# Neighbourhood attention: project queries and keys of both head pairs first, then run one pipeline of attention steps

## What is computed

```python
def na_project(p, qk_gain):
    q = rms_norm(p[0].reshape(B, T, NA_HEADS, HEAD_DIM), qk_gain[0])
    k = rms_norm(p[1].reshape(B, T, NA_HEADS, HEAD_DIM), qk_gain[1])
    v = p[2].reshape(B, T, NA_HEADS, HEAD_DIM)
...
    # for each grid row: queries against a window of 8 x 16 grid keys and all context keys
    s_loc = jnp.einsum('bchd,brcjhd->bhcrj', q_r, k_w).astype(jnp.float32) * NA_SCALE + bias
    s_ctx = jnp.einsum('bchd,bkhd->bhck', q_r, k_ctx).astype(jnp.float32) * NA_SCALE
    p = jax.nn.softmax(jnp.concatenate([s_loc, s_ctx], -1), axis=-1)
    out = p_loc @ v_w + p_ctx @ v_ctx
```

## Time and profile before

| | |
|---|---|
| Median of 3 runs | 2172.21 us (2169.93 to 2174.93) |
| The profiled execution | 2174.71 us, of which the span of the trace is 2172.9 |
| TensorE (PE) busy | 2046.5 us, 94% |
| Weight loads (PEld) | 1689.9 us, 78% |
| VectorE (DVE) busy | 1139.5 us, 52% |
| ScalarE (ACT) busy | 757.2 us, 35% |
| GpSimd (POOL) busy | 645.1 us, 30% |
| Layer 0, neighbourhood attention with its queries and keys | about 60 to 178 us of the span |
| Layer 1, the same | about 1290 to 1389 us |

### The profile page before, as it was taken

One profiled execution on the slowest core, in us unless ns is written; L12 is line 12 of the kernel. 1 busy time (PEld: TensorE's weight loads), 2 busy tenths in 40 slices (PEclk: granted clock), 3 DMA queues, 4 the chain that ended last, 5 costly groups with the idle time before them and its releaser, 6 DMA issues.

```text
span 2172.9 us, 29749 instructions
## 1 busy us (share of the span) xinstructions
PE 2046.5 (94%) x11694; PEld 1689.9 (78%) x11694; DVE 1139.5 (52%) x1975; ACT 757.2 (35%) x1209; POOL 645.1 (30%) x820
## 2 busy tenths in 40 slices
PE   7889999999989999999999998889989989999999
PEld 5777888766668888888888877688866667888887
DVE  5455433578866666277537564654368864212111
ACT  4443232546653211111111244433366643222222
POOL 1111221210002433343333431122220014555555
PEclk8999999999999999999999999997999999999999
DMA  7302431100002333233223210111110002333323
GB/s 295 114 20 72 154 97 40 48 30 10 10 11 68 112 121 100 75 129 133 88 97 117 97 59 30 32 49 40 49 49 10 10 21 78 97 97 97 99 95 107
DMA packets 76528, 166.24 MB, mean 77 GB/s; under 512 B 5224, under 2 KB 46824, under 8 KB 75376
## 3 DMA queue, kind: packets, MB, share of 16 engines
q1 hardware_dynamic: 75728, 163.18, 22.5%
q10 hardware_dynamic: 672, 1.25, 0.2%
HBM read 162.31 MB, written 2.10 MB: 76 GB/s over the span
## 4 chain that ended last, share of the span: by engine, by line
PE 81%; DVE 7%; ACT 4%; issue 4%; DMA 1%; PEld 1%; POOL 1%; SPq 0%; PEldq 0%; DVEq 0%; ACTq 0%; POOLq 0%
PE psum L1156 23%; PE psum L1157 22%; PE psum L1158 22%; PE psum L1415 1%; DMA wm<-w_mod 1%; PE psum L1769 1%; PE psum L1207 1%; ACT nap L771 1%; PE psum L1799 1%; PE psum L1406 1%; POOL wlo L584 1%; PE psum L1538 1%; PE psum L1475 1%; PE psum L1524 1%; PE psum L1476 1%
## 5 line engine op out<-in xcount | busy, mean ns | idle before, releaser
L584 POOL TENSOR_TENSOR wlo<-raw,whi 128x256 fp32r<-128x256 f32 x816 | 644.9, 822 | 1519.8 <-ACT whi L609 1519.8
L1156 PE MATMUL psum<-hhi,whi 128*128 128x512 f32 (+1 forms) x1704 | 611.5, 359 | 15.5 <-DVEq L1970 8.3
L1157 PE MATMUL psum<-hlo,whi 128*128 128x512 f32 (+1 forms) x1704 | 601.3, 353 | 0.0
L1158 PE MATMUL psum<-hhi,wlo 128*128 128x512 f32 (+1 forms) x1704 | 600.7, 353 | 0.0
L609 ACT ACTIVATE whi<-raw 128x1024 fp32r<-128x1024 f32 x204 | 215.6, 1058 | 870.9 <-PE psum L1158 864.2
L1156 PEld LDWEIGHTS psum<-hhi,whi 128*128 128x128 f32 x1704 | 325.5, 191 | 69.9 <-issue 13.5
L1158 PEld LDWEIGHTS psum<-hhi,wlo 128*128 128x128 f32 x1704 | 324.7, 191 | 44.5
L1157 PEld LDWEIGHTS psum<-hlo,whi 128*128 128x128 f32 x1704 | 325.5, 191 | 42.0 <-issue 0.5
L2621 DVE TENSOR_TENSOR ffuf<-ffsa,psum 128x768 f32<-128x768 f32 (+1 forms) x44 | 36.1, 821 | 312.7 <-ACT ffsa L1106 306.0
L2606 DVE SCALAR_TENSOR_TENSOR ffmacc<-wm,csil,ffmacc 128x256 f32<-128x256 f32 x336 | 188.6, 602 | 10.0 <-DVE ffmacc L2606 4.9
L1156 PE MATMUL psum<-uhi,whi 128*128 128x512 f32 (+1 forms) x528 | 188.4, 357 | 3.7 <-DVE ulo L2625 2.1
(11 more groups left out here) (323 smaller groups left out, 3064.5 us busy)
## 6 DMA issues: line engine op xcount, KB each, us to landing
raw<-w_stream SPq DMA_DIRECT2D x204, 512.0 KB, 3.5
wm<-w_mod SPq DMA_DIRECT2D x80, 512.0 KB, 4.0
wm<-w_mod SPq DMA_DIRECT2D x8, 1024.0 KB, 13.1
xres<-x_t SPq DMA_DIRECT2D x8, 384.0 KB, 7.2
out<-xres SPq DMA_DIRECT2D x8, 256.0 KB, 2.7
namask<-c_f ACTq DMA_DIRECT2D x2, 384.0 KB, 3.7
consts<-c_f SPq DMA_DIRECT2D x1, 254.0 KB, 2.8
narpb<-rpb ACTq DMA_DIRECT2D x2, 120.0 KB
```

Source lines behind the costliest of these rows:

```text
L584: nc.gpsimd.tensor_tensor(wlo[:, q % 2, c:c + UW // 4], raw[:, q % RAW, c:c + UW // 4], whi[:, q % 2, c:c + UW // 4], ALU.subtract).then_i ...
L1156: mm(dst, ah, bh, start=first, stop=False)
L1157: mm(dst, ah, bl, start=False, stop=False)
L1158: return mm(dst, al, bh, start=False, stop=last)
```

## The change

Queries and keys of pair 1 are projected right behind those of pair 0, and both barriers between the pairs go. Then a single pipeline runs over the steps of both pairs: 24 in layer 0 and 16 in layer 1.

- `qhi`, `qlo`, `khi` and `klo` hold both pairs (`[P, 2, TOK]`), and steps carry their pair `pr`. To make room the tiles of the stage are laid out anew: `sq`, `t` and `vt` share the place of the outputs' neighbours, and `r`, `mask` and `ks` share another; two unused gaps shrink or move.
- `na_second` replaces `na_pair`. TensorE multiplies the grid part of unit 4, then the sums of pair 0's key squares, then the context part of unit 4 (layer 0), the grid part of unit 5, the sums of pair 1's query squares, the context part of unit 5, the sums of pair 1's key squares, and then the 40 filler matmuls, now into bank 5. Pair 1's keys go to PSUM pair 0 and its query sums to PSUM pair 3.
- A new semaphore `na_scaled` is counted up by VectorE when a query or key has been scaled out of PSUM. TensorE waits for it before unit 4 (pair 0's queries), before pair 1's query sums (pair 0's keys) and before the filler (pair 1's queries). ScalarE waits for it before the roots of pair 1.
- ScalarE rounds unit 5 before the roots of pair 0's keys instead of behind them, and squares pair 1's queries before it rounds unit 6.
- SyncE's two waits for a phase count become 2 and 4, since two barriers of a layer are gone.

```diff
@@ -307,7 +305,7 @@
                     steps = []
                     for kind, t in att_blocks(l):
                         for a in range(2):
-                            steps.append((s, b, kind, t, a))
+                            steps.append((s, b, kind, t, a, pr))
                             s += 1
                         b += 1
                     plan[l, pr] = steps
...
@@ -345,6 +343,10 @@
         def NAQK(l, pr, part):
 
             return 3 * (2 * l + pr) + ("q", "kx", "kc").index(part) + 1
+
+        def SCALED(l, pr, part):
+
+            return 4 * l + 2 * pr + ("q", "k").index(part) + 1
 
         NAK_PARTS = (("kx", slice(CTX_LEN, TOK)), ("kc", slice(0, CTX_LEN)))
 
...
@@ -548,14 +550,14 @@
             for h in range(2 * MOD_HEAD, 2 * MOD_GATE):
                 load_mod(0, h)
             loads(RAW, ML_G + RAW)
-            sp.wait_ge(pe_phase, 4)
+            sp.wait_ge(pe_phase, 2)
             for n in range(MOD_GATE, MODC):
                 for h in range(2 * n, 2 * n + 2):
                     load_mod(0, h)
                 if n < MOD_ML:
                     load(ML_G + RAW + n - MOD_GATE)
             loads(ML_G + RAW + MOD_ML - MOD_GATE, FF0 + 4)
-            sp.wait_ge(pe_phase, 6)
+            sp.wait_ge(pe_phase, 4)
             for j in range(HG):
                 for h in range(2 * MODN(j), 2 * MODN(j) + 2):
                     load_mod(1, h)
...
+                his(u + 4)
                 for part, cs in NAK_PARTS:
                     act.wait_ge(ev_ps, NAQK(l, 0, part))
                     rsqrt_of(NA["ks"][:, 1, cs], psum_pair(psum, 1)[:, cs], 1.0 / HEAD_DIM).then_inc(rs2, 1)
-                his(u + 4)
-
-            def na_pair(l, pr, full):
-                u, q0 = u0(l, NA_QK) + 2 * pr, 0 if full else CTX_LEN
+
+            def na_second(l, full):
+                u, q0 = u0(l, NA_QK) + 2, 0 if full else CTX_LEN
                 act.wait_ge(w_used, u + 1)
+                A(NA["sq"][:, q0:], psum_pair(psum, 2)[:, q0:], ACT.Square).then_inc(sq2, 1)
                 his(u + 3)
-                A(NA["sq"][:, q0:], psum_pair(psum, 2)[:, q0:], ACT.Square).then_inc(sq2, 1)
-                act.wait_ge(nak_x, 2 * l + pr + 1)
-                A(NA["ks"][:, 0, CTX_LEN:], psum_pair(psum, 3)[:, CTX_LEN:], ACT.Square).then_inc(sq2, 1)
-                act.wait_ge(ev_ps, NAQK(l, pr, "q"))
-                rsqrt_of(NA["r"][:, q0:], psum_pair(psum, 0)[:, q0:], 1.0 / HEAD_DIM).then_inc(rs2, 1)
+                act.wait_ge(nak_x, 2 * l + 2)
+                A(NA["ks"][:, 0, CTX_LEN:], psum_pair(psum, 0)[:, CTX_LEN:], ACT.Square).then_inc(sq2, 1)
+                act.wait_ge(ev_ps, NAQK(l, 1, "q"))
+                act.wait_ge(na_scaled, SCALED(l, 0, "q"))
+                rsqrt_of(NA["r"][:, q0:], psum_pair(psum, 3)[:, q0:], 1.0 / HEAD_DIM).then_inc(rs2, 1)
                 act.wait_ge(w_used, u + 2)
-                A(NA["ks"][:, 0, 0:CTX_LEN], psum_pair(psum, 3)[:, 0:CTX_LEN], ACT.Square).then_inc(sq2, 1)
+                A(NA["ks"][:, 0, 0:CTX_LEN], psum_pair(psum, 0)[:, 0:CTX_LEN], ACT.Square).then_inc(sq2, 1)
+                act.wait_ge(na_scaled, SCALED(l, 0, "k"))
                 for part, cs in NAK_PARTS:
-                    act.wait_ge(ev_ps, NAQK(l, pr, part))
+                    act.wait_ge(ev_ps, NAQK(l, 1, part))
                     rsqrt_of(NA["ks"][:, 1, cs], psum_pair(psum, 1)[:, cs], 1.0 / HEAD_DIM).then_inc(rs2, 1)
                 his(u + 4)
 
 
-            def att_act(l, pr):
-                steps = PLAN[l, pr]
-
-                def exp_of(s, b, kind, t, a):
+            def att_act(l):
+                steps = PLAN[l, 0] + PLAN[l, 1]
+
+                def exp_of(s, b, kind, t, a, pr):
...
@@ -1124,12 +1128,10 @@
                 full = l < DEPTH - 1
                 norm_phase(l, 0, True)
                 na_inputs(l, full)
-                for pr in range(2):
-                    if pr:
-                        na_pair(l, pr, full)
-                    barrier(u0(l, NA_QK) + 2 * pr + 2)
-                    att_act(l, pr)
-                    barrier(u0(l, NA_QK) + 2 * pr + 2)
+                na_second(l, full)
+                barrier(u0(l, NA_OUT))
+                att_act(l)
+                barrier(u0(l, NA_OUT))
                 his(u0(l, ML_G))
                 barrier(u0(l, ML_G))
                 ml_act(l, full)
...
@@ -1370,29 +1372,35 @@
                         ins.then_inc(w_used, 1)
                     if g == (12 if l else 9):
                         na_sums(l, 0, "q", 0 if l else 1, NA["sq"], ranges(full))
+
+            def na_second(l, full):
+                u = u0(l, NA_QK) + 2
+                unit(u)
+                pe.wait_ge(na_scaled, SCALED(l, 0, "q"))
+                feature_unit(u, 2, [(CTX_LEN, TOK)], done=not full)
                 na_sums(l, 0, "kx", 1, NA["ks"][:, 0, :], [(CTX_LEN, TOK)])
                 na_sums(l, 0, "kc", 1, NA["ks"][:, 0, :], [(0, CTX_LEN)])
+                if full:
+                    feature_unit(u, 2, [(0, CTX_LEN)])
+                unit(u + 1)
                 if l == 0:
                     pe.wait_ge(mod_add, 3)
-                keep_warm(40)
-
-            def na_pair(l, pr, full):
-                u = u0(l, NA_QK) + 2 * pr
-                unit(u)
-                feature_unit(u, 2, ranges(full))
-                unit(u + 1)
-                feature_unit(u + 1, 3, [(CTX_LEN, TOK)], done=False).then_inc(nak_x, 1)
-                na_sums(l, pr, "q", 0, NA["sq"], ranges(full))
-                feature_unit(u + 1, 3, [(0, CTX_LEN)])
-                na_sums(l, pr, "kx", 1, NA["ks"][:, 0, :], [(CTX_LEN, TOK)])
-                na_sums(l, pr, "kc", 1, NA["ks"][:, 0, :], [(0, CTX_LEN)])
-                keep_warm(40)
-
-
-            def att_pe(l, pr):
-                steps = PLAN[l, pr]
-
-                def scores(s, b, kind, t, a):
+                pe.wait_ge(rs2, NAQK(l, 0, "q"))
+                feature_unit(u + 1, 0, [(CTX_LEN, TOK)], done=False).then_inc(nak_x, 1)
+                pe.wait_ge(na_scaled, SCALED(l, 0, "k"))
+                na_sums(l, 1, "q", 3, NA["sq"], ranges(full))
+                feature_unit(u + 1, 0, [(0, CTX_LEN)])
+                pe.wait_ge(rs2, NAQK(l, 0, "kc"))
+                na_sums(l, 1, "kx", 1, NA["ks"][:, 0, :], [(CTX_LEN, TOK)])
+                na_sums(l, 1, "kc", 1, NA["ks"][:, 0, :], [(0, CTX_LEN)])
+                pe.wait_ge(na_scaled, SCALED(l, 1, "q"))
+                keep_warm(40, bank(5)[:, 0:256])
+
+
+            def att_pe(l):
+                steps = PLAN[l, 0] + PLAN[l, 1]
+
+                def scores(s, b, kind, t, a, pr):
 
                     if s >= 4:
                         pe.wait_ge(s_nmx, s - 2)
...
@@ -1937,13 +1945,11 @@
                 full = l < DEPTH - 1
                 norm_phase(l, 0, True)
                 na_inputs(l, full)
-                for pr in range(2):
-                    if pr:
-                        na_pair(l, pr, full)
-                    barrier()
-                    att_pe(l, pr)
-                    keep_warm(13)
-                    barrier()
+                na_second(l, full)
+                barrier()
+                att_pe(l)
+                keep_warm(13)
+                barrier()
                 out_units(l, 0, NA_OUT, 2, tiles_of(NA["ohi"]), tiles_of(NA["olo"]), ranges(full))
...
@@ -2083,14 +2089,17 @@
                         add_square(l, 1, full, m - 1)
 
 
-            def na_query(l, full):
+            def na_query(l, pr, full):
 
                 q0, t = 0 if full else CTX_LEN, NA["t"]
-                seq(V.scalar_tensor_tensor(t[:, q0:], psum_pair(psum, 2)[:, q0:], lc[:, l, C_NAQ:C_NAQ + 1],
-                                           NA["r"][:, q0:], ALU.mult, ALU.mult))
-                parts = [(query_order(NA["qhi"], e), query_order(NA["qlo"], e), grid_order(t, e)) for e in range(2)]
+                qhi, qlo = NA["qhi"][:, pr, :], NA["qlo"][:, pr, :]
+                dve.wait_ge(rs2, NAQK(l, pr, "q"))
+                V.scalar_tensor_tensor(t[:, q0:], psum_pair(psum, 2)[:, q0:], lc[:, l, C_NAQ:C_NAQ + 1],
+                                       NA["r"][:, q0:], ALU.mult, ALU.mult).then_inc(na_scaled, 1)
+                dve.wait_ge(na_scaled, SCALED(l, pr, "q"))
+                parts = [(query_order(qhi, e), query_order(qlo, e), grid_order(t, e)) for e in range(2)]
...
@@ -2100,16 +2109,18 @@
 
             def na_key(l, pr):
 
+                src, khi, klo = psum_pair(psum, 0 if pr else 3), NA["khi"][:, pr, :], NA["klo"][:, pr, :]
                 for part, cs in NAK_PARTS:
                     dve.wait_ge(rs2, NAQK(l, pr, part))
-                    ins = V.scalar_tensor_tensor(NA["t"][:, cs], psum_pair(psum, 3)[:, cs], lc[:, l, C_NAK:C_NAK + 1],
+                    ins = V.scalar_tensor_tensor(NA["t"][:, cs], src[:, cs], lc[:, l, C_NAK:C_NAK + 1],
                                                  NA["ks"][:, 1, cs], ALU.mult, ALU.mult)
-                seq(ins)
```

(28 more changed lines are left out.)

61 lines of the change are left out of this document (33 added, 28 removed).

## The result

The changed kernel took 2143.31 us, the median of 4 runs (2140.38 to 2145.97), against 2171.07 us, the median of 4 runs of the kernel before: a ratio of 0.9883, with a 95% interval of 0.9867 to 0.9899. It is faster by 27.8 us; the forecast was 27.5 us and 2144.7 us. Two more comparisons of the same kernel gave 0.9882 (0.9857 to 0.9907) and 0.9891 (0.9874 to 0.9907). The profiled execution took 2141.4 us; its span is 2139.6.

The account below looks back on a forecast made before the run. VectorE was taken to limit most of the merged pipeline's second half. Savings of 11.5 + 8.4 + 7.6 = 27.5 us took the 2172.21 us median to 2144.7 us; range 2139.5 to 2153.0.

Parts of the forecast that it names:

- Hand-over: Between pair 0's projection and first scores, pair 1's first unit replaces idle and filler, hiding pair 0's key chain: 11.5 us saved.
- One pipeline instead of two: Attention of both pairs merged: 60.7 to 52.3 us in layer 0, 49.7 to 42.1 in layer 1; saves 8.4 and 7.6.
- from the first score to the step that begins at 110.82, 18.05 us as before: Layer 0's merged attention, its start up to that VectorE step: unchanged from the old kernel at 18.05 us.
- 4.4 + 23.0 + 6.8: Rest of layer 0's merged attention: two steps 4.4 us, twelve more steps 23.0, last VectorE step to next stage 6.8.
- Rival B: Clock falls at the second pair's context steps, whole second half at the lower level: 7.4 us lost, 2152.1 us; chance 0.12.
- D: Clock falls in the merged pipeline and stays low into output and next projections: slower than before, 2189.7 us; chance 0.01.
- VectorE as the limit: In most of the merged pipeline's second half VectorE sets the pace, 4.3 us for two grid steps.
- the ring of TensorE and ScalarE: In the attention's grid steps, ScalarE and TensorE together need 4.2 us for two steps, below VectorE's 4.3.
- Rival C: Hand-over hides nothing, pair 1's units late or pair 0's key chain exposed: only 16.0 us saved, 2156.2 us; chance 0.04.
- E: VectorE not the limit, ScalarE's 1.95 us holds in 16 grid steps: 3.3 us more saved, 2141.4 us; chance 0.05.
- F: Second pair's scores are held by a wait, no pipelining: 2160.7 us and up to no change; chance 0.02.

Follow-up runs that it names:

- values_even: Changed kernel with both halves of the products with the values multiplied in TensorE's even steps: 2135.21 us, ratio 0.9859 to the kernel before.

## Why the prediction was right, and where it was not

**Hand-over.** Right in each step. The first scores came 25.93 and 22.56 us after unit 3's end, forecast 25.9 and 22.7. Pair 0's key chain was hidden: in layer 1 its key scaling ended at 1301.16 us, 3.0 us before the query sums that wait for it. No wait for a lower weight part stands before unit 5. Without the hand-over, 10.7 us are lost.

**One pipeline instead of two.** Right in sum, 16.1 us against 16.0. Layer 1 took 41.86 us three times, forecast 42.1. In layer 0 the forecast's 52.3 us took over the low stretch of the earlier trace rows as if it had one length; it is 51.47 with 3.4 us of low clock and 54.9 with 13.7, which came in two of three profiles, and the 6.8 us of the earlier trace rows lie between, as 52.3 does. The term that was mis-sized is "from the first score to the step that begins at 110.82, 18.05 us as before": to the same step, VectorE's eleventh maximum, it took 20.9 us in the first profile, 17.5 in the second and 21.0 in the third. From there to the output projection it took 34.0 us each time, forecast 4.4 + 23.0 + 6.8 = 34.2. The term should have carried a bound of 3 us. The trace of the kernel before had the warning: two attention parts of layer 0 with the same work, 29.6 and 31.1 us, and a second low stretch that is longer than that of the earlier trace rows, 10.2 us in all:

```profile
148.00:152.00 4.00, 1.30 (x4) 0.58 (x4) 2.24 (x12) 2.87 (x9) 0.09 (x1) 0.67 0.41 133
152.00:156.00 4.00, 3.77 (x22) 2.93 (x23) 2.40 (x9) 2.88 (x9) 0.00 (x0) 0.50 0.00 0
156.00:160.00 4.00, 3.79 (x22) 3.31 (x22) 1.91 (x7) 2.33 (x6) 0.00 (x0) 0.55 0.00 0
```

So the forecast's sentence that the clock came back to full within 4 us each time was a misreading, and so is its use against rivals B and D: the earlier trace rows themselves give 6.8 us. And that the merging came to 16.1 us where 16.0 were forecast is in part luck, since it hangs on which low stretches the two profiles drew.

**VectorE as the limit.** Wrong as to the engine, right as to the size. The merged half runs at 4.21 us for two steps, set by the ring of TensorE and ScalarE, which the forecast named with 4.2 and put second. VectorE's own figure was 4.155, not 4.3. The forecast's 4.3 is 2.05 + 2.37 - 0.1, from two steps of the kernel before. In `values_even`, which VectorE paces, such a pair takes 1.92 and 2.24 us (maxima at 1336.31, 1338.23 and 1340.47): nearly all of the difference is in the shorter step, where the lower half starts 0.24 us behind the output's lower part, and 0.36 in the kernel before. Eight steps at 4.3 instead of 4.21 are 0.4 us, so the sum did not show it.

**Rival B** (the clock falls in the second half, 2152.1 us) did not come. The second pair's context steps kept 1.00 with TensorE busy 7.51 of 8.50 us, and the grid steps behind them kept it with 11.07 of 13.50. The Trainium skill's rule on micro-idles between groups of matmuls ("TensorE: Matmul & The Clock Gate", section "A second HAM failure mode: psum-queue depth-cycling") was not borne out by these rows. The clock did fall where the idle times are long, in front of the first transposes, 1.40 us busy in 4.00. **Rival C** is excluded by the hand-over's figures, **E** by the 4.21 us, **F** by the seams (no idle between the pairs), and **D** by the full clock at the output projection.

**The total.** 27.8 us measured and 27.5 forecast agree better than their parts do. The two stretches give 25.3 to 28.8 us against the first profile of the kernel before and 26.0 to 29.5 against the second; the rest lies in stretches that the change does not touch, most of it in the third of the table. That the total hit within 0.3 us is luck. The comparisons of the changed kernel gave 27.8, 27.4 and 25.1 us.

## What to carry to other kernels

Where two equal pipelines run one after the other, price their merging by the ends: the fill and drain of one, its barriers and one fall of the clock, here 8 us each time. When two engines seem to limit a loop, take the load off each and off both. A pace of 4.21 with 4.155 right behind it means that relieving one of them is worth 0.06 us at the most (here 0.01 us for VectorE and 0.06 for the ring), and relieving both 0.3 us. Where an engine with a gated clock must wait at the start of a pipeline, filler in those waits can be cheap: here the attention got shorter and took the same time, within 0.02 us, in two profiles.
